# One core, two transformer blocks in fp32: the compression of block columns with parted operands, 60 stationary columns, three weight chunks

## What is computed

```python
CMP_BLOCK = 32; CMP_STRIDE = 16; CMP_HIDDEN = 256; HEAD_DIM = 64   # s = 256, g = 2 groups

def compress(t, pos_emb, w1, b1, w2):
    b, s, g, d = t.shape
    chunks = t.reshape(b, s // CMP_STRIDE, CMP_STRIDE, g, d)
    blocks = jnp.concatenate([chunks[:, :-1], chunks[:, 1:]], axis=2)
    blocks = blocks + pos_emb[None, None, :, None, :]
    flat = jnp.moveaxis(blocks, 3, 2).reshape(b, -1, g, CMP_BLOCK * d)
    return jax.nn.gelu(flat @ w1 + b1) @ w2
```

## Time and profile before

| | us |
|---|---|
| median of 3 runs | 1892.61 (1888.31 to 1893.77) |
| profiled execution | 1893.45 |
| its span, first to last instruction | 1891.7 |

### The profile page before, as it was taken

How to read it: one execution, slowest core, us unless ns; L and a number is a source line. 1 busy time by engine, 2 the same in 40 slices (tenths; PEclk the granted TensorE clock), 3 DMA queues, 4 the chain that set the end, 5 groups by cost and what they waited for, 6 DMA issues and landing times.

```text
span 1891.7 us, 30382 instructions
## 1 busy us (share of the span) xinstructions
PE 1809.4 (96%) x11888; PEld 1601.3 (85%) x11888; DVE 1099.8 (58%) x2037; ACT 889.2 (47%) x1403; POOL 223.0 (12%) x112
## 2 busy tenths in 40 slices
PE   6999999999899989999999999899989999998988
PEld 6999898888789988999797988799979887777876
DVE  7555464446655556555562548555567885583764
ACT  5444433564444345443443564444455554463564
POOL 1000000555300000000001635200000000001000
PEclk9999999999999998999999999999989999799999
DMA  7454555533445444454446334445435443104421
GB/s 279 186 190 176 178 200 190 212 134 134 178 167 184 181 166 155 189 185 181 178 177 258 134 138 163 172 173 200 169 133 199 167 167 134 67 1 155 179 101 56
DMA packets 29901, 311.60 MB, mean 165 GB/s; under 512 B 3312, under 2 KB 3696, under 8 KB 4848
## 3 DMA queue, kind: packets, MB, share of 16 engines
q1 hardware_dynamic: 28944, 307.16, 43.6%
q0 software_dynamic: 864, 3.15, 0.5%
HBM read 309.24 MB, written 1.05 MB: 164 GB/s over the span
## 4 chain that ended last, share of the span: by engine, by line
PE 84%; DVE 7%; ACT 4%; issue 3%; DMA 1%; POOL 0%; SPq 0%; DVEq 0%; ACTq 0%
PE psum L833 82%; PE psum L840 2%; DMA ring<-in_weights 1%; ACT region_r L462 1%; DVE ring_r L468 1%; ACT Sb L1678 1%; DVE Sb L2199 1%; DVE xs L2099 0%; DVE region L2341 0%; DVE x L2106 0%; DVE PTs L2310 0%; DVE region L2402 0%; DVE region L2398 0%; POOL ring_r L468 0%; DVE xs L2067 0%
## 5 line engine op out<-in xcount | busy, mean ns | idle before, releaser
L462 ACT ACTIVATE region_r<-ring 128x1024 fp32r<-128x1024 f32 x483 | 504.0, 1054 | 385.4 <-PE psum L833 369.7
L468 DVE TENSOR_TENSOR ring_r<-ring,region_r 128x1024 fp32r<-128x1024 f32 x431 | 514.0, 1220 | 184.9 <-ACT region_r L462 170.3
L833 PE MATMUL psum<-hH,region_r 128*128 128x256 f32 x2256 | 562.2, 287 | 7.1 <-POOL xs_r L474 3.7
L833 PE MATMUL psum<-xs_r,region_r 128*128 128x256 f32 x2240 | 550.5, 283 | 0.0
L833 PEld LDWEIGHTS psum<-hH,region_r 128*128 128x128 f32 x2256 | 428.2, 190 | 21.2 <-issue 11.1
L833 PEld LDWEIGHTS psum<-xs_r,region_r 128*128 128x128 f32 x2240 | 425.3, 190 | 4.8 <-issue 0.5
L833 PE MATMUL psum<-hH,ring_r 128*128 128x256 f32 x2336 | 324.7, 280 | 0.0
L833 PEld LDWEIGHTS psum<-hH,ring_r 128*128 128x128 f32 x2336 | 298.1, 189 | 0.1
L833 PE MATMUL psum<-region_r 128*128 128x512 f32 x872 | 295.4, 395 | 2.1 <-DVE region_r L2146 2.1
L468 POOL TENSOR_TENSOR ring_r<-ring,region_r 128x1024 fp32r<-128x1024 f32 x52 | 114.8, 2227 | 1038.9 <-ACT region_r L462 1021.9
L833 PEld LDWEIGHTS psum<-region_r 128*128 128x128 f32 x872 | 163.9, 188 | 37.2 <-DVE region_r L2146 2.5
(11 more groups left out here) (235 smaller groups left out, 1899.3 us busy)
## 6 DMA issues: line engine op xcount, KB each, us to landing
ring<-in_weights SPq DMA_DIRECT2D x192, 1536.0 KB, 6.4
gpost<-in_posts POOLq DMA_DIRECT2D x6, 512.0 KB, 5.4
cst<-in_const SPq DMA_DIRECT2D x1, 1198.0 KB, 23.0
xs<-in_mem SPq DMA_DIRECT2D x1, 1024.0 KB, 5.5
x<-in_x SPq DMA_DIRECT2D x1, 1024.0 KB, 7.6
out<-x SPq DMA_DIRECT2D x2, 512.0 KB, 2.6
pars<-in_par SPq DMA_DIRECT2D x1, 368.0 KB, 8.0
p<-in_par SPq DMA_DIRECT2D x1, 206.0 KB, 24.3
```

Source lines behind the costliest of these rows:

```text
L462: eng.activation(unit.high, unit.raw, ACT.Copy).then_inc(h_ready, 1)
L468: eng.tensor_tensor(unit.low, unit.raw, unit.high.bitcast(F32), ALU.subtract).then_inc(l_ready, 1)
L833: ins = pe.matmul(bank, lhsT, rhs, start=start, stop=stop)
```

## The change

Both operands of the compression's first product are parted. After the eight additions of a side VectorE copies the 30 columns rounded to fp32r and subtracts the copy; both parts lie side by side in `flat_parts`, 60 stationary columns for each of 16 steps. The weights become eight units of `LAYER_SPLIT` (`CMP_UNITS`, four a side, in places of their own) with high parts by ScalarE and low parts by VectorE. TensorE streams the high and then the low part of each unit's weights over the 60 columns: 32 fp32r matmuls a side. The result has 60 rows, high columns in rows 0 to 29 and low columns in 30 to 59; `hidden_turned` adds them while it transposes, by a product with `pair`, two stacked identities. The eight units are packed in three full chunks instead of four; a second empty chunk takes the fourth's place in the count, so the gates' chunks come one earlier.

```diff
@@ -61,15 +61,15 @@
 
 CHUNK, SLOTS = 3072, 4
 
-ACT_OWN, DVE_OWN = 26, 119
+ACT_OWN, DVE_OWN = 26, 121
 
 TWO_PI = (6.28125, 0.0019350051879882812, 3.0199159795e-07)
 PI_BELOW = 3.1415925
 MTILE = KD * P
 
 
-FFN_CHUNKS, A_CHUNKS, B_CHUNKS, C_CHUNKS, D_CHUNKS = FT, 8, 1, 3, 4
-GATE_CHUNKS, BRANCH_CHUNKS, OUT_CHUNKS = 8, 4, 3
+FFN_CHUNKS, A_CHUNKS, B_CHUNKS, C_CHUNKS, D_CHUNKS = FT, 8, 1, 3, 3
+GATE_CHUNKS, EMPTY_CHUNKS, BRANCH_CHUNKS, OUT_CHUNKS = 8, 2, 4, 3
 AT_FFN1 = 0
 AT_C = FFN_CHUNKS
 AT_A = AT_C + C_CHUNKS
@@ -77,7 +77,7 @@
 AT_D = AT_B + B_CHUNKS
 AT_GATE = AT_D + D_CHUNKS
 AT_EMPTY = AT_GATE + GATE_CHUNKS
-AT_BRANCH = AT_EMPTY + 1
+AT_BRANCH = AT_EMPTY + EMPTY_CHUNKS
 AT_OUT = AT_BRANCH + BRANCH_CHUNKS
 AT_FFN2 = AT_OUT + OUT_CHUNKS
 LAYER_CHUNKS = AT_FFN2 + FFN_CHUNKS
@@ -104,10 +104,12 @@
 N_FFN, N_A, N_B, N_GATE, N_OB, N_OA = 3 * FT, 24, 3, 24, 24, 8
 EARLY_GATES = 4
 AB_UNITS = [*range(U_A, U_A + N_A), *range(U_B, U_B + N_B)]
+CMP_UNITS = [*range(3 * AT_D, 3 * AT_D + 8)]
+CMP_PLACES = [("gate", 0), ("gate", 1), ("gate", 2), ("cmp", 0)] + [("ring", n) for n in range(4)]
 GATE_UNITS = [*range(U_GATE, U_GATE + N_GATE)]
 BRANCH_UNITS = [*range(U_BRANCH, U_BRANCH + N_BRANCH)]
 OUT_UNITS = [*range(U_OUT, U_OUT + N_OUT)]
-LAYER_SPLIT = [*range(U_FFN1, U_FFN1 + N_FFN), *AB_UNITS, *GATE_UNITS, *BRANCH_UNITS, *OUT_UNITS,
+LAYER_SPLIT = [*range(U_FFN1, U_FFN1 + N_FFN), *AB_UNITS, *CMP_UNITS, *GATE_UNITS, *BRANCH_UNITS, *OUT_UNITS,
                *range(U_FFN2, U_FFN2 + N_FFN)]
 
 
@@ -145,6 +147,8 @@
 
 def place(u):
 
+    if u in CMP_UNITS:
+        return CMP_PLACES[u - CMP_UNITS[0]]
     for kind, first, n in (("gate", U_GATE, N_GATE), ("branch", U_BRANCH, N_BRANCH)):
         if first <= u < first + n:
             return kind, (u - first) % PLACES
@@ -160,6 +164,8 @@
 def held_before(u):
 
     kind, at = place(u)
+    if u in CMP_UNITS:
+        return U_FFN1 + N_FFN - 1
     if kind == "out":
         return GATE_UNITS[-1] if at < 3 else BRANCH_UNITS[-1]
     if kind == "even_out":
...
@@ -605,6 +611,10 @@
                       act_r[:, :, :, :].rearrange("p a b t -> p (a b t)"),
                       region_r[:, at_q:at_q + UNIT]]
 
+        cmp_highs = [gpost_r[:, 0, :]]
+        flat_parts = region_r[:, at_y + CF * SEQ:at_y + CF * SEQ + 2 * 16 * 4 * NCMP]\
+            .rearrange("p (c j h n) -> p c j h n", c=2, j=16, h=2)
+
         def tiles_of(ap, n):
             return ap.rearrange("p (k t) -> p k t", k=n)
 
...
@@ -1171,9 +1182,10 @@
                     split_feature(Job("gate", m, b), U_GATE + n)
                     if b == 2:
                         used.append(w_used[(AT_GATE + m) % SLOTS])
-                    if n == 3 * GATE_CHUNKS - 3:
-                        chunk(AT_EMPTY)
-                        used.append(w_used[AT_EMPTY % SLOTS])
+                    if n in (3 * GATE_CHUNKS - 3, 3 * GATE_CHUNKS - 2):
+                        empty = AT_EMPTY + n - (3 * GATE_CHUNKS - 3)
+                        chunk(empty)
+                        used.append(w_used[empty % SLOTS])
 
                 def hidden_turned(c):
 
@@ -1181,19 +1193,26 @@
                     job = Job("hidT", c)
                     job.wait_empty(pe)
                     for m in range(2):
-                        turn(job.bank[:, m * P:(m + 1) * P], usb[:, c, m * P:(m + 1) * P], job.full if m else None)
+                        mm(job.bank[:, m * P:m * P + 2 * NCMP], usb[0:4 * NCMP, c, m * P:(m + 1) * P],
+                           C("pair")[0:4 * NCMP, :], True, True, job.full if m else None)
 
                 for c in range(2):
-                    Job("kc" if c == 0 else "vc", 0).wait_emptied(pe)
+                    pe.wait_ge(flat_ready, 2 * lay[0] + c + 1)
                     job = Job("hid", c)
                     job.wait_empty(pe)
-                    for jj in range(16):
-                        if jj % 8 == 0:
-                            w = chunk(AT_D + 2 * c + jj // 8)
-                        mm(job.bank[0:2 * NCMP, 0:256], flat[:, c, jj, :, :].rearrange("p g n -> p (g n)"),
-                           w[:, jj % 8 * 256:(jj % 8 + 1) * 256], jj == 0, jj == 15, job.full if jj == 15 else None)
-                        if jj % 8 == 7:
-                            used.append(w_used[(AT_D + 2 * c + jj // 8) % SLOTS])
+                    for n in range(4):
+                        u = CMP_UNITS[4 * c + n]
+                        unit = Split(u)
+                        for part, (ready, w) in enumerate(((h_ready, unit.high), (l_ready, unit.low))):
+                            pe.wait_ge(ready, unit.count)
+                            for j in range(4):
+                                first, last = n == part == j == 0, n == j == 3 and part
+                                mm(job.bank[0:4 * NCMP, 0:256],
+                                   flat_parts[:, c, 4 * n + j].rearrange("p h n -> p (h n)"),
+                                   w[:, j * 256:(j + 1) * 256], first, bool(last), job.full if last else None)
+                        used.append(h_room)
+                        if u % 3 == 2 or u == CMP_UNITS[-1]:
+                            used.append(w_used[u // 3 % SLOTS])
                 hidden_turned(0)
                 gate_tile(0)
                 hidden_turned(1)
@@ -1727,6 +1746,9 @@
                 for n, (kind, at) in enumerate(MIX_TILES):
                     if 1 <= n < len(AB_UNITS) - HIGHS + 1:
                         high_part(act_, AB_UNITS[n + HIGHS - 1])
+                    if n >= len(MIX_TILES) - 2:
+                        for u in CMP_UNITS[2 * (n - len(MIX_TILES) + 2):][:2]:
+                            high_part(act_, u)
                     job = Job(kind, at)
                     if kind == "u":
                         copy(job, usb[:, at % 2, :], job.bank[:, 0:SEQ])
@@ -1735,14 +1757,17 @@
                     elif kind == "qm":
                         copy(job, qmT[:, at, :], job.bank[:, 0:SEQ])
                 for i in range(NT):
+                    for u in CMP_UNITS[4:6] if i == 0 else CMP_UNITS[6:7]:
+                        high_part(act_, u)
                     job = Job("tok", i)
                     job.wait_full(act_)
                     own(act_.activation(vtok[:, i, :], job.bank[:, 0:2 * P], ACT.Copy))
                     copy(job, gate[:, i, :], job.bank[:, 2 * P:2 * P + 24], ACT.Sigmoid)
+                high_part(act_, CMP_UNITS[7])
                 Job("cg", CF - 1).wait_emptied(act_)
                 for c in range(2):
                     job = Job("hid", c)
-                    copy(job, usb[0:2 * NCMP, c, :], job.bank[0:2 * NCMP, 0:256])
+                    copy(job, usb[0:4 * NCMP, c, :], job.bank[0:4 * NCMP, 0:256])
                     if c == 0:
                         for u in GATE_UNITS[:3]:
                             high_part(act_, u)
@@ -2276,6 +2301,9 @@
                 for n, (kind, at) in enumerate(MIX_TILES):
                     if 1 <= n < len(AB_UNITS) - HIGHS + 1:
                         low_part(dve, AB_UNITS[n + HIGHS - 1])
+                    if n >= len(MIX_TILES) - 2:
+                        for u in CMP_UNITS[2 * (n - len(MIX_TILES) + 2):][:2]:
+                            low_part(dve, u)
                     job = Job(kind, at)
                     if kind == "cg":
 
@@ -2314,10 +2342,19 @@
                                         ins.then_inc(job.free, 1)
                                     else:
                                         own(ins)
+                        job.wait_emptied(dve)
+                        own.settle()
+                        whole = flat[:, c].rearrange("p j g n -> p j (g n)")
+                        own(dve.tensor_copy(flat_parts[:, c, :, 0, :], whole))
+                        own.settle()
+                        dve.tensor_tensor(flat_parts[:, c, :, 1, :], whole, flat_parts[:, c, :, 0, :].bitcast(F32),
+                                          ALU.subtract).then_inc(flat_ready, 1)
                     rotated()
                     if (kind, at) in ROPED:
                         pending.append((kind, at))
 
+                for u in CMP_UNITS[4:]:
+                    low_part(dve, u)
                 add = C("cmp_add").rearrange("p (i n) -> p i n", i=NT)
                 one = C("cmp_one").rearrange("p (i n) -> p i n", i=NT)
                 for i in range(NT):
@@ -2843,6 +2880,7 @@
     seen = (ends[None, None, :] <= token.reshape(NT, P, 1)).transpose(1, 0, 2).reshape(P, -1)
     c["cmp_add"], c["cmp_one"] = np.where(seen, 0.0, NEG), seen
     c["upto"], c["ones"] = reach[:P, :P], np.ones((P, P))
+    c["pair"] = np.concatenate([np.eye(2 * NCMP)] * 2 + [np.zeros((P - 4 * NCMP, 2 * NCMP))])
     rotate = np.zeros((P, P))
     inv = np.zeros((P, 1))
     freq = THETA ** (-np.arange(ROT) * 2.0 / (2 * ROT))
@@ -2920,10 +2958,12 @@
     rows += groups(tiles, 3)
     columns_b = np.r_[kv0 + 3 * P:kv0 + 4 * P, kv0 + 5 * P:kv0 + 6 * P, g0:g0 + 24]
```

(10 more changed lines are left out.)

1 line of the change is left out of this document (added).

## The result

| | before | changed |
|---|---|---|
| median of the runs, us | 1893.19 (1888.31 to 1894.53) | 1872.39 (1867.51 to 1877.83) |
| profiled execution, us | 1893.45 | 1868.50 |
| its span, us | 1891.7 | 1866.7 |
| mean granted clock | 0.976 | 0.977 |

The ratio is 0.9896, interval 0.9857 to 0.9934: 20.8 us faster, where the forecast was 8.3 and the range ended at 1880.5. The direction was right and the size was not. (The two profiled executions differ by 24.95 us, since that of the changed kernel was one of its fastest; the medians are what counts, the traces say where.)

A forecast was written before the change was run, and what follows sets the result against it. TensorE, busy in 96% of the span, was taken as the bound, with VectorE ahead of the stage and a DMA behind it. Profiled 1893.45 us less 4.5 and 3.8, median 0.84 lower, gave 1884.3; range 1880.5 to 1889.5.

The forecast's parts named there:

- Everything else shifts with the gain: Past the `v` matmuls and the later chunks, the rest of the program only moves earlier, with no further gain or loss.
- The stage: Compression's first product: 64 matmuls in 7.5 us instead of 14.0, 6.5 us less a layer, loads of 60 columns hidden.
- VectorE ahead of it: Copy and subtraction of `kc` ahead of the `vc` additions delay TensorE's next tile by 1.15 us, bounds 1.05 and 1.45.
- The landing: The gates' first weight chunk lands 6.1 us after issue in layer 0 and 7.6 in layer 1, at 329.3 and 1023.8.
- Landing to `v` matmuls: From the gate chunk's landing, ScalarE's work takes 5.85 us before the `v` matmuls can start.
- The `v` matmuls: Behind the compression they start at 335.15 instead of 339.67 and 1029.6 instead of 1033.42, gains of 4.5 and 3.8 us.
- The clock: Rival: new idle gaps lower TensorE's clock, some 3.4 us lost, giving the late landing's 1888.8 us; chance 0.17 together.
- The rival of loads that aren't hidden: Compression's first product takes 15.4 us, 1.4 more than before; 2.5 us a layer slower, 1897.7 us; chance 0.04.
- The sum: Whole kernel: 1893.45 us less 4.5 and 3.8 is 1885.15, with the median 0.84 lower 1884.3.

The follow-up runs named there:

- e1: The kernel before with an unused 128-byte buffer behind the constants, no instruction changed: 1876.49 us, ratio 0.9922.
- e3: The changed kernel itself, measured once more beside other runs on one chip: 1870.65 us, ratio 0.9889.
- e2: The changed kernel with the stacked identities in their own buffer at the very end, all older buffers at their old addresses: 1884.52 us, ratio 0.9962.
- e7: The kernel before with a gap of 128 bytes right behind `hH`, the input's high part: 1878.72 us, ratio 0.994.
- e9: The kernel before with a gap of 128 bytes directly ahead of `region`, so that only `region` moves: 1878.82 us, ratio 0.9941.
- e4: The changed kernel with the copy and subtraction of `kc` moved behind the `vc` additions: 1872.08 us, ratio 0.9898.
- e11: The kernel of e2 with the copy and subtraction of `kc` behind the `vc` additions, as in e4: 1882.86 us, ratio 0.995.
- e12: The changed kernel with 32 bytes more behind the constants, 160 bytes in all: 1880.08 us, ratio 0.9944.
- e14: The kernel of e2 with a gap of 128 bytes ahead of `region`, as in e9: 1870.82 us, ratio 0.9885.
- e15: The same kernel as e2, run again for its profile: 1885.38 us, ratio 0.9972.
- e13: The kernel before with 128 bytes ahead of the weight ring, so the ring and all buffers behind it move together: 1894.23 us, ratio 1.0014.
- e10: The kernel before with 128 bytes behind the constants and 128 more ahead of `region`, which moves by 256: 1893.53 us, ratio 1.0016.

## Why the prediction was wrong, and where it was right

**The step that failed** is "Everything else shifts with the gain". The constants' 30 more columns appear in no term of the sum and were thereby counted at nothing. They move everything behind them by 128 bytes against the ring, and the pace of TensorE in all stages depends on that. The term was worth 13.0 us alone at the old compression (e1), and 18.9 - 5.0 = 13.9 at the new one (e3 against e2). The low pass is 9.5 to 10 us of that (busy time of its group 324.7 before, 315.2 in e1, 314.6 in the changed kernel). The rest goes by the layout: in e1 the 4480 matmuls of the high passes have 0.9 ns less, some 4 us; in e7 and e9, which gain 13.7 and 12.4 us, they have not, but the matmuls with both operands in `region` have 2.8 us less. No row of the trace before could have given the size, since none shows a second layout. What could have been seen is that every weight tile reads its high part from `region` and its low part from the ring, and that the diff changes their distance; that calls for a wide range, not for a zero.

**The stage**, forecast 7.5 us for 64 matmuls: the first starts at 319.33 and the last group of four at 326.34, so with four spacings of 0.117 it is 7.48 us. A load of 60 columns has 132 ns (forecast 133, from the line between two rows) and is hidden.

**VectorE ahead of it**, forecast 1.15 us and 1.6 idle: 0.42 and 0.66 with gaps, 1.1 in all, and 1.55 idle. The gapped destination doesn't lose the copy's faster pace, as the lower of the two bounds had it; the rule of the Trainium skill (VectorE: DVE Perf Modes, "What auto-detection actually checks") that was weighed there holds in this row.

**The landing**, forecast 6.1 and 7.6 us after issue: 6.32 and 6.42. The layer 1 value was copied from one row of before and was 1.2 us too long. Landing to `v` matmuls, forecast 5.85: 332.50 - 326.45 = 6.05.

**The `v` matmuls**, forecast gains 4.5 and 3.8. Layer 0: 339.67 - 332.50 = 7.17, of which 293.62 - 290.99 = 2.63 was there ahead of VectorE's stage; that leaves 4.54. Layer 1: 1033.42 - 1015.46 = 17.96. The tile behind `vc` started at 987.50 instead of 999.32 in spite of VectorE's 1.1 us more, so 12.9 was there ahead of that; that leaves 5.0, and the 1.2 beyond the forecast is the landing. (This way of counting gives 4.4 for layer 0.) The tile's start:

```profile
987.50 15.36 PE psum L844 x124
```

**The clock**, a rival at 0.17 together with a late landing: it happened, after a fashion. Among the profiled executions of the eight kernels and repeats with the new compression (changed, e2, e3, e4, e11, e12, e14, e15) six of the 16 `v` stages ran 3.4 us or so at the lower level, 1.5 us lost each; of the old compression's, none of 18 (nine kernels). It isn't bound to the old places (e4 and e12 have others). That is some 0.6 us a layer on average, where the rival had 3.4 for one. The rival of loads that aren't hidden didn't come true.

**The sum.** The compression alone is worth 5.0 and 4.3 us where the layout is left as it was (e2, e15, with three drops of 1.5 us in the four stages of their profiled executions), 5.8 with the places of the change (e1 to e3, measured together), and 6.5 to 10.6 where `region` alone is moved (e9 to e14, which were not measured together; no drop in these four traces). The forecast gain of 8.3 lies between, and all of these lie within the forecast range of gains, 3.1 to 12.1. Up to the `v` matmuls the part that was argued holds term by term, and gives 9.5 us in the two layers; that the whole kernel shows less in the closest comparisons, 4.3 to 5.8 by the medians, is in part the drops of the clock and otherwise open. The range failed by a term that wasn't on the list.

**What stays open.** Why a pass that reads only `ring_r` and `hH` goes by the distance from the ring to `region`. Work of other engines beside it is one candidate, since ScalarE and VectorE read the ring and write or read `region` at the same time; and the products of e7 and e9 whose own operands kept their distance and still went faster speak for it. Against it, those engines' own operations have the same mean in every layout looked at (1220 to 1221 ns for VectorE's low parts and 1054 to 1055 for ScalarE's high parts in the kernel before, e1, e7, e9 and e13). No run stops the other engines, so the candidate isn't tested. The Trainium skill (SBUF — State Buffer, "SBUF: two separate sides") says that among the engines only the port pair shared by GpSimd and VectorE causes waits, and that TensorE never waits on anyone. No run here shows TensorE waiting on another engine, but a pace that hangs on a distance between buffers isn't what one would take from that sentence, and the measurement decides. Only shifts of 32, 64, 128, 160 and 256 bytes were run.

What brings on the drop of the clock behind the shorter compression is open too; the idle time ahead of the tile behind `vc` isn't needed for it (e11). The Trainium skill (TensorE: Matmul & The Clock Gate, "What's actually happening") has the chip look at activity in windows that run freely, not aligned with the kernel; that agrees with a drop that comes in layer 0 of e2 and not in layer 0 of the same kernel's repeat, but no run here proves it. And no version was found that clearly beats the changed kernel; e4 and e14 equal it.

## To carry to other kernels

A diff that makes a buffer longer, if only by 30 constants, moves each buffer behind it, and here that was worth more than the idea of the change. So list which buffers move against which, and price a change of layout with a wide range. And test it apart: add the same bytes as an empty buffer to the kernel before, and take them out of the changed one; one run each tells what belongs to the change, and a few gaps of 32 to 256 bytes are a cheap thing to try in a kernel that is bound by TensorE.

## What the runs showed of the hardware

- TensorE's pace in a long run of matmuls at full clock depends on where SBUF buffers lie relative to each other. The same 2336 fp32r matmuls, 128 stationary columns and 256 moving, went at 118.3 ns or at 113.4 to 113.9, by a shift of 128 bytes of the buffer of high weight parts against that of the low parts. A shift of 256 bytes, or of both, left 118.3 (117.8 in e10); 64 bytes made the whole kernel 0.5% slower.
- The matmul's spacing stays above its columns in every layout: 256 columns at 2.4 GHz are 107 ns, and the best here was 113.4 with 128 stationary columns and 117 with 60.
- The product with `pair`, four records of 60 rows and 30 moving columns a side, takes 0.63 us (2.5 us over the 16 of both layers), and a record's mean is 276 ns, about that of one over 256 columns.
- Executions of one kernel differ in the clock that TensorE is granted, with the same work. e2 dropped to the lower level in both `v` stages and e15 in one, 1.5 us each, and from 1600 to 1660 us they had 0.74 and 0.80 of the full clock, which goes with 3.0 us in that stretch of the program. The busy time just ahead, 2.91 us in each of the two windows shown, doesn't tell the drop of e2 from the full clock of the changed kernel; more pairs weren't compared.
